# One kernel, two changes in four places: the first weight unit of a layer on x times the norm's weights, and half of h's low parts on GpSimd

## What is computed

```
def rmsnorm(x, g):
    y = xf * lax.rsqrt(jnp.mean(xf * xf, axis=-1, keepdims=True) + EPS)
    return (y * g.astype(jnp.float32)).astype(x.dtype)
...
    h = rmsnorm(x, norm_g) * (1.0 + scale[:, None, :]) + shift[:, None, :]
...
    gq, gk, gv, glr, sq, sk, sv, gate = _split(h @ in_w, ODD_SIZES)
...
def swiglu(h, w_gate, w_up, w_down):
    return (jax.nn.silu(h @ w_gate) * (h @ w_up)) @ w_down
```

## Time and profile before

| | us |
|---|---|
| median of 3 runs | 989.41 (989.23 to 990.48) |
| the profiled execution | 992.07 |
| its span, first to last instruction | 990.3 |
| PE busy in it | 954.0 (96%) |
| DVE, ACT, POOL busy | 714.2, 507.6, 41.8 |

### The profile page before, as it was taken

How to read it: one execution, slowest core, us unless ns; L and a number is a source line. 1 busy time by engine, 2 the same in 40 slices (tenths; PEclk the granted TensorE clock), 3 DMA queues, 4 the chain that set the end, 5 groups by cost and what they waited for, 6 DMA issues and landing times.

```text
span 990.3 us, 17238 instructions
## 1 busy us (share of the span) xinstructions
PE 954.0 (96%) x7025; PEld 876.7 (89%) x7025; DVE 714.2 (72%) x994; ACT 507.6 (51%) x745; POOL 41.8 (4%) x68
## 2 busy tenths in 40 slices
PE   6999999999999999999999999999999999999998
PEld 6799999989799789999778888889998978898987
DVE  4778877767866766576899988977988765465554
ACT  4654364456544446544755456474646454444444
POOL 2100000000000003320100000000000000000000
PEclk9999999999999999999999999999999999999999
DMA  9987586844875894658378887776534457474731
GB/s 363 384 279 257 184 290 234 297 167 150 273 248 183 287 302 153 234 214 300 84 242 270 292 276 251 265 251 216 153 124 126 153 170 234 149 262 143 253 110 43
DMA packets 134247, 219.43 MB, mean 222 GB/s; under 512 B 8585, under 2 KB 100090, under 8 KB 134168
## 3 DMA queue, kind: packets, MB, share of 16 engines
q1 hardware_dynamic: 132416, 214.99, 64.9%
q0 software_dynamic: 992, 1.76, 0.7%
q10 hardware_dynamic: 760, 1.59, 0.4%
HBM read 217.25 MB, written 1.05 MB: 220 GB/s over the span
## 4 chain that ended last, share of the span: by engine, by line
PE 75%; DVE 11%; DMA 6%; issue 4%; ACT 4%; SPq 0%; ACTq 0%; DVEq 0%
PE pw L569 50%; PE pacc L569 24%; DMA ring<-in_odd_in_w 3%; DVE ACC L1676 3%; DVE WL L1660 2%; ACT WH L1175 1%; ACT AR L1175 1%; DMA ring<-in_ada_w 1%; DVE SQT L1756 1%; DVE hl L1761 1%; PE pw L1022 1%; DMA ring<-in_odd_out_w 1%; DMA ring<-in_ffn_w_down 1%; ACT hh L1175 1%; DMA cst<-in_consts 1%
## 5 line engine op out<-in xcount | busy, mean ns | idle before, releaser
L1175 ACT ACTIVATE WH<-ring 128x1024 fp32r<-128x1024 f32 x288 | 302.6, 1057 | 300.1 <-PE pw L569 125.0
L1660 DVE TENSOR_TENSOR WL<-ring,WH 128x1024 fp32r<-128x1024 f32 x288 | 348.0, 1224 | 90.8 <-ACT WH L1175 90.1
L569 PE MATMUL pacc<-YH,WH 128*128 128x256 f32 x672 | 192.9, 287 | 2.6 <-issue 1.7
L569 PE MATMUL pw<-hh,WH 128*128 128x256 f32 x704 | 187.8, 288 | 4.4 <-ACT AR L1175 2.1
L569 PE MATMUL pacc<-YH,WL 128*128 128x256 f32 x672 | 190.1, 283 | 0.0
L569 PE MATMUL pacc<-YL,WH 128*128 128x256 f32 x672 | 190.1, 283 | 0.0
L569 PE MATMUL pw<-hh,WL 128*128 128x256 f32 x704 | 184.9, 284 | 0.0
L569 PE MATMUL pw<-WH,hh 128*128 128x512 f32 x448 | 177.0, 395 | 4.4 <-DVE WL L1660 4.0
L569 PE MATMUL pw<-WL,hh 128*128 128x512 f32 x448 | 174.9, 390 | 0.0
L569 PEld LDWEIGHTS pw<-hh,WH 128*128 128x128 f32 x704 | 135.7, 193 | 9.2 <-issue 6.3
L569 PE MATMUL pw<-hl,WH 128*128 128x256 f32 x704 | 142.7, 284 | 0.0
(11 more groups left out here) (272 smaller groups left out, 782.2 us busy)
## 6 DMA issues: line engine op xcount, KB each, us to landing
ring<-in_w_mod SPq DMA_DIRECT2D x72, 512.0 KB, 5.6
ring<-in_odd_in_w SPq DMA_DIRECT2D x56, 512.0 KB, 6.0
ring<-in_ada_w SPq DMA_DIRECT2D x48, 512.0 KB, 6.8
ring<-in_ffn_w_gate SPq DMA_DIRECT2D x88, 256.0 KB, 3.6
ring<-in_ffn_w_up SPq DMA_DIRECT2D x88, 256.0 KB, 4.5
ring<-in_ffn_w_down SPq DMA_DIRECT2D x44, 512.0 KB, 5.1
ring<-in_even_in_w SPq DMA_DIRECT2D x40, 512.0 KB, 7.4
ring<-in_even_out_w SPq DMA_DIRECT2D x16, 512.0 KB, 6.4
```

The source lines that it names most:

```text
L569: return eng.matmul(o, a, b, start=start, stop=stop, skip_group_check=True)
L1175: return eng.activation(dst, src, func, **kw)
L1660: tt(WL[:, i % NL, :], slot(half_of(i)), WH[:, i % NH, :].bitcast(F32), SUB).then_inc(s_lo, 1)
```

## The change

At the start of L_ODD, L_F1, L_MIX and L_F2:

- **The first unit** (qk0, f1g0, wu0, f2g0; new function `first`) multiplies x * GS instead of h: ACT writes `hh` from xT with GS as its scale (`early`), DVE the low part (`early_lows`), behind each quarter of the update. Two more columns of `hh`, the shift, give sh @ W in the same matmuls (258 columns). PE sums half of the squares ahead of it, behind the last quarter, half after its second chunk, and spreads the root after its fifth chunk. When it is read, DVE multiplies by the root (`unnormed`, from `RB`, an ACT copy of the bank r) and ACT adds sh @ W as a bias (`offsets` copies it to `ES`).
- **h itself** is made from the root on, while that unit runs: chunks 0 to 3 as before; chunks 4 to 7 with the shifted value kept in SQT by a further ACT instruction, rounded by a second one, and subtracted on GpSimd (`lows`).
- f1g0, f1u0, f2g0 and f2u0 are units of `cols_T` instead of two halves of a gate and up pair, which spares the first transposition (`turn(0)`). `xnew` is spread after f1u0, and the side lists of L_F1 start after it. `side.flush()` on DVE stands ahead of the update instead of behind it.
- The ada units keep away from the layers' ends: `weave` leaves 5 units at the end and 3 at the start of a layer free instead of 3 and 0, and the units in `QUIET` do no ada work. The `warm` matmuls at the four places are gone; one ACT table load is issued ahead of L_ODD's start, another among L_ODD's output units.

```diff
-    def weave(side, from_, clear=0):
+    def weave(side, from_, clear=0, lead=0):
...
-            while k < len(side) and (2 * k + 1) * (len(main) - clear) <= 2 * i * len(side):
+            while k < len(side) and (2 * k + 1) * (len(main) - clear - lead) <= 2 * (i - lead) * len(side):
...
-            if b < 11:
+            if b == 0:
+                cols(f"{tag}g0", Wg, 0)
+                cols(f"{tag}u0", Wu, 0)
+            elif b < 11:
                 pair(f"{tag}g{b}", Wg, Wu, 0, 256 * b)
                 pair(f"{tag}u{b}", Wg, Wu, 512, 256 * b)
...
-    weave(ada(a0, 2, 3) + ada(a1, 0, 2), at, 3)
+    weave(ada(a0, 2, 3) + ada(a1, 0, 2), at, 5)
...
-    weave(ada(a1, 2, 3) + ada(a2, 0, 4), at, 3)
+    weave(ada(a1, 2, 3) + ada(a2, 0, 4), at, 5, 3)
...
-    weave(ada(a2, 4, 8), at, 3)
+    weave(ada(a2, 4, 8), at, 5, 3)
...
-        else:
+        elif nm not in quiet:
...
+QUIET = ("eo7", "qk0", "qk1", "oo7", "f1g0", "f1u0", "f1d10", "wu0", "wu1", "wo3", "f2g0", "f2u0", "f2d10")
...
+                def rest():
+                    sums(2)
+                    sums(3)
+                    full[f"fin{L}"] = (s_sqr, sqr_n[0])
+
+                later[L] = rest
+
...
-            def norm_mod(L, z):
-                ada("tail " + TAIL[L - 1])
-                back(f"fin{L - 1}")
-                if L >= L_MIX:
-                    warm(5, f"warm{L}a")
-                spread(f"r{L}", 0, z, (s_u, 8 * L + 8), True)
-                warm(4, f"warm{L}b")
...
+            def first(L, z, c=0):
...
+                name = FIRST[L]
+                k, a = unit(name)
+                names = early_names(L)
+                bks = [open_(nm, None, True) for nm in names]
+                for half in range(2):
+                    H, Lo = piece(2 * k + half, a)
+                    for kk in range(4):
+                        i = 4 * half + kk
+                        if i == 2:
+                            later[L - 1]()
+                            back(f"fin{L - 1}")
+                        if i == 5:
+                            spread(f"r{L}", c, z, (s_rb, L), True)
+                        p.wait_ge(s_eh, 8 * (L - 1) + i + 1)
+                        for m, pb in enumerate(bks):
+                            mm(pb[:, 0:T + 2], H[:, kk, m * P:m * P + P], hh[:, i, :], i == 0, False)
+                            mm(pb[:, 0:T + 2], Lo[:, kk, m * P:m * P + P], hh[:, i, :], False, False)
+                        p.wait_ge(s_el, 8 * (L - 1) + i + 1)
+                        for m, pb in enumerate(bks):
+                            last = mm(pb[:, 0:T + 2], H[:, kk, m * P:m * P + P], hl[:, i, :], False, i == 7)
+                    last.then_inc(s_use, 1)
+                for nm in names:
+                    full[nm] = used(name)
+                    back(nm)
                 back(f"r{L}")
...
+            def early(L, sh, c):
+
+
+                s.wait_ge(s_gs, L + 1)
+                s.wait_ge(*gone[f"ada{c}"])
+                s.wait_ge(*used(LAST_H[L]))
+                act(hh[:, :, T:T + 2], shift_cols(sh)).then_inc(s_esh, 1)
+                for q in range(4):
+                    ns = (2 * q, 2 * q + 1)
+                    if q == 3:
+                        cut_on(L - 1)
+                        squares(L - 1, ns)
+                    for n in ns:
+                        s.wait_ge(s_x, X_FIN[L - 1] + n + 1)
+                        act(hh[:, n, 0:T], xT[:, n, :], scale=GS[:, n:n + 1]).then_inc(s_eh, 1)
+                    if q < 3:
+                        squares(L - 1, ns)
+                k = unit(FIRST[L])
+                cut(2 * k)
+                modulate(L, sh, range(4))
+                cut(2 * k + 1)
+                for n in range(4, 8):
+                    s.wait_ge(s_u, 8 * L + n + 1)
+                    s.wait_ge(*used(FIRST[L], 1))
+                    h = SQT[:, n, :]
+                    s.wait_ge(*s.step(act(h, h, ACT.Identity, bias=sh[:, n:n + 1])))
+                    act(hh[:, n, 0:T], h).then_inc(s_hh, 1)
+                act(RB[L], pw[place[f"r{L}"]][:, 0:T]).then_inc(s_rb, 1)
+
+            def offsets(L, scale=1.0):
+                for m, nm in enumerate(early_names(L)):
+                    s.wait_ge(*full[nm])
+                    act(ES[:, m:m + 1], pw[place[nm]][:, T:T + 1], scale=scale).then_inc(s_es, 1)
...
+            def early_lows(L, ks):
+                for k in ks:
+                    v.wait_ge(s_eh, 8 * (L - 1) + k + 1)
+                    stt(out=hl[:, k, 0:T], in0=xT[:, k, :], scalar=GS[:, k:k + 1], in1=hh[:, k, 0:T].bitcast(F32),
+                        op0=MUL, op1=SUB).then_inc(s_el, 1)
...
+            def modulate(L, sh, ks, lows):
...
+            def between(L, g, sh, root):
+
+
+                v.wait_ge(s_esh, L)
+                tt(hl[:, :, T:T + 2], shift_cols(sh), hh[:, :, T:T + 2].bitcast(F32), SUB)
+                update(L - 1, g, lambda q: early_lows(L, (2 * q - 2, 2 * q - 1)))
+                k = unit(FIRST[L])
+                cut(2 * k)
+                root()
+                early_lows(L, (6, 7))
+                mods[0] += 1
+                modulate(L, sh, range(4), True)
+                modulate(L, sh, range(4, 6), False)
+                cut(2 * k + 1)
+                modulate(L, sh, range(6, 8), False)
+
+            def unnormed(L, dsts):
+                v.wait_ge(s_rb, L)
+                for m, nm in enumerate(early_names(L)):
+                    v.wait_ge(s_es, 2 * (L - 1) + m + 1)
+                    tt(dsts[m], RB[L], pw[place[nm]][:, 0:T], MUL).then_inc(s_bank[place[nm]], 1)
...
+            side.flush()
             half_gate(8, M2[:, 16:24])
...
+            def lows(L):
+
+
+                for k in range(4, 8):
+                    g.wait_ge(s_hh, 8 * L + k + 1)
+                    eng.tensor_tensor(hl[:, k, 0:T], SQT[:, k, :], hh[:, k, 0:T].bitcast(F32), SUB).then_inc(s_hlp, 1)
...
-            g.wait_ge(*used("oo7"))
+            g.wait_ge(*used("oo1"))
             for i, nm in enumerate(("ssm_b_re_2", "ssm_b_im_2")):
```

More of the change, by code:

```diff
@@ L864, in _ @@
                         close(last, f"lw{q}")
-            for j in range(2, 4):
-                cols_T(L_ODD, f"qk{j}")
+            cols_T(L_ODD, "qk3")
             cols_N(L_ODD, "gv")
@@ L982, in s5_weights @@
             def s5_weights():
-                yield from idle(6)
+                yield from idle(10)
                 p.wait_ge(s_cm, 2)
@@ L1039, in ffn @@
                                  finish(L) if blk == 11 else None, (lambda: turn(blk)) if blk < 11 else None)
-            def xnew_back():
-                yield from idle(3)
-                back("xnew")
-                yield
-            ada("tail oo7")
-            back("fin1")
-            warm(6, "warm2a")
-            spread("r2", 10, 4, (s_u, 24), True)
-            spread("xnew", 8, 4, None, True)
-            warm(5, "warm2b")
-            back("r2")
-            side.gens.append(xnew_back())
-            side.rate = 1
+            side.rate = 0
             side.gens.append(s5_weights())
+            first(L_F1, 4, 10)
             ffn(L_F1, "f1", Y_F1)
             side.flush()
-            norm_mod(L_MIX, 5)
             def s5_in(h):
@@ L1102, in _ @@
             side.rate = 0
-            for j in range(2):
-                cols_T(L_MIX, f"wu{j}", [(s_ura, j + 1), (s_urd, j + 1)])
+            first(L_MIX, 5)
+            cols_T(L_MIX, "wu1", [(s_ura, 2), (s_urd, 2)])
             s5_in(0)
@@ L1312, in _ @@
                 pieces(f"eo{j}")
-            squares(L_EVEN)
-            cut_on(L_EVEN)
-            modulate(L_ODD, M1[:, 0:8])
             eng.preload_act_table_set("natural_log_exp_and_others")
+            early(L_ODD, M1[:, 0:8], 3)
+            offsets(L_ODD, float(P) ** -0.5)
+            for m, nm in enumerate(early_names(L_ODD)):
+                s.wait_ge(*gone[nm])
+                q2 = GQ[:, m * T:m * T + T]
+                act(q2, q2, ACT.Identity, scale=float(P) ** -0.5, bias=ES[:, m:m + 1]).then_inc(s_q0, 1)
             def decay():
@@ L1512, in ffn @@
             def ffn(tag, y0, n0):
-                for blk in range(12):
+                L = L_F1 if tag == "f1" else L_F2
+                offsets(L)
+                for m, nm in enumerate(early_names(L)):
+                    s.wait_ge(*gone[nm])
+                    act(fbuf(0, m), fbuf(0, m), ACT.Silu, bias=ES[:, m:m + 1]).then_inc(s_sl, 1)
+                pieces(f"{tag}u0")
+                if L == L_F1:
+                    evac("xnew", XNW, src=pw[place["xnew"]][:, 0:T])
+                    side.rate = 1
+                for blk in range(1, 12):
                     if blk < 11:
@@ L1582, in _ @@
             side.rate = 0
-            for nm in ("wu0", "wu1", "wc0", "wv0"):
+            offsets(L_MIX)
+            for m, nm in enumerate(early_names(L_MIX)):
+                s.wait_ge(*gone[nm])
+                act(UT[:, m, :], UT[:, m, :], ACT.Identity, bias=ES[:, m:m + 1]).then_inc(s_ut, 1)
+            s.wait_ge(s_ut, 2)
```

(36 more changed lines are left out.)

203 lines of the change are left out of this document (115 added, 88 removed).

## The result

| | before | after |
|---|---|---|
| median, us | 989.89 (989.23 to 990.48, 4 runs) | 1010.88 (1010.01 to 1014.71, 4 runs) |
| ratio | | 1.022, 95% interval 1.0192 to 1.0247 |
| the profiled execution's span, us | 990.3 | 1008.6 |
| mean granted clock | 0.996 | 0.987 |

A forecast was written before the change was run, and what follows sets the result against it. The prediction took PE's matmuls at their pace as the bound, with 5.8 us of hole at L_F2's start. Terms -0.8 - 2.3 - 2.0 + 3.5 + 1.0 + 2.0 = +1.4 gave 990.8 us, range 985 to 997.

The forecast's parts named there:

- L_F2's start: Third unit at T + 17.9, T being the end of the last output matmul of the layer ahead: -0.8 us.
- The update chain: At L_F2's start DVE needs 1.76 us a quarter against PE's 1.44, so the last update comes at T + 1.0.
- the late spread: At L_F2's start the root's spread comes near 791.4 us, 2.6 later than before.
- the starved second unit: At L_F2's start the second unit waits for h's later chunks from ACT and GpSimd, ending near T + 16.2.
- L_ODD's and L_F1's starts: L_ODD -2.3 us, with the low clock there gone; L_F1 -2.0, with sums moved behind the output quarters and a transposition spared.
- L_MIX, +3.5: At L_MIX's start twelve copies wait for the first unit's late result: `s5_in(0)` +2.0 us, and 1.5 for a low clock.
- Ada units, +2.0: Sixteen ada units in 25 units instead of 30 take more DVE time: +1.5 us, and +0.5 in L_ODD.
- Clear slots and two columns more of 258 are put at nothing: Clear slots at layer ends and the two extra columns lie beside PE's units or cost under 0.05 us a unit.
- s5_skip, +1.0: At L_F1's end this DVE step of 2.82 us comes later, delaying the low part for the last output unit: +1.0 us.
- D: Rival: first units wait for `hh` as long as before, so the starts gain nothing; 999 us, chance 0.05.
- B: Rival: second units fed in drips, clock falling at two more starts, DVE the bound in L_F1; 997.7 us, chance 0.2.

The follow-up runs named there:

- e18: Changed kernel with none of the four new layer starts and the ada units of L_ODD and L_F1 in the old order (the left-overs only): 996.38 us, ratio 1.0062.
- e19: Changed kernel with L_F1 and L_MIX starting as before and the ada units of L_ODD and L_F1 in the old order: 994.22 us, ratio 1.0045.
- the ladder: Runs adding the change's parts in turn to the kernel before, each less its own runs of before: from 6.7 us (left-overs only) to 21.0 (the change).
- e9: Changed kernel with L_MIX's start as before and the ada units of L_ODD and L_F1 in the old order: 994.80 us, ratio 1.005.
- e3: Changed kernel with the ada units of L_ODD and L_F1 in the old order: 1004.85 us, ratio 1.016.
- e4: Kernel before with only the change's four `weave` lines, the new order of the ada units: 996.33 us, ratio 1.0076.
- e7: Changed kernel with L_MIX's start as in the kernel before: 1003.79 us, ratio 1.0138.
- e1: Kernel before with rows of hh and hl 258 words long instead of 256: 991.16 us, ratio 1.0016.

## Why the prediction was wrong

- **L_F2's start: right.** T + 17.4 for T + 17.9, and with the transposition the layer's first three units are 1.1 shorter in the profile (forecast 0.8). The whole layer takes 198.5 us in e18, without this start, and 197.2 in e19, with it; that its row above says +0.8 is the 512-column pace. The update chain, the late spread, the starved second unit and GpSimd's 0.69 us (I took 0.7, between 0.44 and 1.5) are in the trace. The Trainium skill, page "GPSIMD Engine Reference", section 3.1, gives 1.96 times DVE's time for a two-input operation on 2048 elements. On 256 the trace has 0.69 against the 0.44 of DVE's form, 1.6 times: it agrees that GpSimd is slower, and for this size the measured 1.6 holds.
- **L_ODD's and L_F1's starts: right where they stand.** What follows L_ODD's first two units and 24 matmuls on 16 weight columns starts 2.6 sooner after T (T + 18.9 for T + 21.5; forecast 2.3), PEclk is 1.00 at its start, and L_ODD's output units take 1.6 less without the sums between them, or 1.25 against e18, whose output matmuls have the same pace (forecast 1.2). By the ladder, though, the three starts together are worth some 2 us and not 5.1: part of the gain did not stay. The one profile of e9, which has L_F1's start too, is 2.6 shorter than e19's in L_ODD and 3.0 longer in L_F1. That a gain at a start is a loan where DVE and the ring are bound a few units later is my reading and not shown.
- **L_MIX, +3.5: the mechanism was right and two terms were mis-sized.** Copies 5.22 instead of 3.32, because I took the row of a PSUM source for an SBUF one, and the low clock over 10 us instead of 3.4, with `s5_in(0)` inside it. +7.3 in the profile, +10.3 by the ladder, +7.4 with the ada units in the new order.
- **Ada units, +2.0: the step that failed.** I counted DVE's passes and never asked what the order does to the transfers, though the windows had the column for it. 6.1 us by e3 and 6.4 by e4. The place was wrong too: the prediction put 1.5 of its 2.0 in L_F1, while the profiles have 5.2 in L_ODD and 3.4 in L_F1 (e4 against before), or 7.3 and 1.4 (e7 against e9).
- **"Clear slots and two columns more of 258 are put at nothing": the other step that failed.** Together with the rest of the left-overs 6.7 us (e18), 1.6 of it the rows (e1). I had priced the two columns by their number, 0.05 us a unit; the cost is in the rows of memory, in 512-column units that have no 258 at all. About 4 us of the other 5 lie in L_F1, and what makes them is read and not run.
- **s5_skip, +1.0: right in kind, and 1.6.** DVE runs it at 683.12 for 2.83 us, right ahead of YL. PE's wait for YL ahead of f1d10:

```profile
686.72 0.39 PE L592 MATMUL pacc<-YH,WH 128*128 128x256 f32 x1 [1.64 <-DVE YL L1789]
```

- **The rivals.** The numbers nearest are D's (999, whose own terms add up to 999.5) and B's (997.7), both with the wrong cause: the first unit did start about 1 us behind T, against D, and the clock did not fall at the second units of L_F1 and L_F2 (PEclk 1.00), it fell in L_MIX and in mid-layer, where the stretch at 324.5 to 331.5 us lies behind the wait that the ada order made. The range ended 14 us too low because no rival had the transfers or the left-overs in it, and its upper end was built from one rival at a time, while order, left-overs and L_MIX came together.
